# Pool weights two groups to a unit, and the rope key's 32 columns outside the units

## The reference

```
h = rmsnorm(x) * (1 + sc1) + sh1
proj = h @ w_in                     # 1024 x 4128: cq 768 | ckv 256 | kr 32 | u 1024 | gates 2048
latent = [rmsnorm(ckv), rope(kr)]   # kr is the key part shared by all heads
q = rmsnorm(cq) @ w_uq
y[g] = window_mean(u[g], width 2, 4, 8, 16) - u[g]      # 4 groups of 256 channels
a_out = concat_g(y[g] @ w_pool[g]) * pool_scale         # w_pool[g] is 256 x 256
mixed = (sigmoid(gates[:1024]) * a_out + sigmoid(gates[1024:]) * attention) @ w_out
```

## Time and profile before

| | |
|---|---|
| median of three runs | 2399.89 us (2397.15 to 2406.32) |
| profiled execution | 2402.1 us, span 2400.3 us |
| TensorE matmul busy | 2294.3 us, 96% |
| VectorE, ScalarE, GpSimd busy | 48%, 36%, 28% |
| mean granted TensorE clock | 0.973 |
| chain that ended last | PE 87%, DVE 4%, ACT 2%, DMA 2%, SP queue 2%, POOL 1% |
| mean DMA rate | 96 GB/s |

### The profile page before, as it was taken

How to read it: one execution, slowest core, us unless ns; L and a number is a source line. 1 busy time by engine, 2 the same in 40 slices (tenths; PEclk the granted TensorE clock), 3 DMA queues, 4 the chain that set the end, 5 groups by cost and what they waited for, 6 DMA issues and landing times.

```text
span 2400.3 us, 43263 instructions
## 1 busy us (share of the span) xinstructions
PE 2294.3 (96%) x16431; PEld 2058.7 (86%) x16431; DVE 1150.5 (48%) x1701; ACT 867.5 (36%) x1864; POOL 666.6 (28%) x328
## 2 busy tenths in 40 slices
PE   6999999999988999999989999999999889999998
PEld 4889998757768999998988898977676789999998
DVE  3342651743345666651152608337334556666433
ACT  4123224732213555541231222267222235555321
POOL 0233433400003333333322234333000223333332
PEclk8999999999999999999989999999999989999999
DMA  8564332033312222236336542321332222222322
GB/s 282 153 209 85 75 81 64 21 97 95 104 36 70 71 85 81 79 100 183 110 115 195 162 84 70 85 58 29 97 96 76 62 62 79 83 83 79 89 82 80
DMA packets 338370, 230.62 MB, mean 96 GB/s; under 512 B 62828, under 2 KB 321701, under 8 KB 338236
## 3 DMA queue, kind: packets, MB, share of 16 engines
q1 hardware_dynamic: 336034, 224.01, 32.5%
q10 hardware_dynamic: 2202, 4.79, 0.6%
HBM read 223.15 MB, written 5.60 MB: 95 GB/s over the span
## 4 chain that ended last, share of the span: by engine, by line
PE 87%; DVE 4%; ACT 2%; DMA 2%; SPq 2%; POOL 1%; issue 1%; DVEq 1%; ACTq 0%
PE PS L1426 57%; PE PS L1394 6%; PE PS L1786 5%; PE PS L1832 5%; PE PS L1703 3%; PE PS L1443 2%; PE PS L1729 2%; POOL wlo L897 1%; PE PS L1508 1%; PE PS L1706 1%; PE PS L1625 1%; PE PS L1680 1%; DMA raw<-w_in 1%; PE PS L1780 1%; PE PS L1755 1%
## 5 line engine op out<-in xcount | busy, mean ns | idle before, releaser
L897 POOL TENSOR_TENSOR wlo<-raw,whi 128x1024 fp32r<-128x1024 f32 (+2 forms) x260 | 596.4, 2295 | 1610.0 <-ACT whi L507 1610.0
L507 ACT ACTIVATE whi<-raw 128x1024 fp32r<-128x1024 f32 (+2 forms) x260 | 260.1, 1001 | 913.5 <-PE PS L1426 714.7
L1426 PE MATMUL PS<-h_hi,whi 128*128 128x288 f32 (+1 forms) x2528 | 549.0, 299 | 17.1 <-POOL wlo L897 17.1
L1426 PE MATMUL PS<-h_lo,whi 128*128 128x288 f32 (+1 forms) x2528 | 544.9, 297 | 0.0
L1426 PE MATMUL PS<-h_hi,wlo 128*128 128x288 f32 (+1 forms) x2528 | 544.6, 297 | 0.0
L1426 PEld LDWEIGHTS PS<-h_hi,whi 128*128 128x128 f32 (+1 forms) x2528 | 408.6, 189 | 30.7 <-POOL wlo L897 18.3
L1426 PEld LDWEIGHTS PS<-h_hi,wlo 128*128 128x128 f32 (+1 forms) x2528 | 409.8, 189 | 0.7
L1426 PEld LDWEIGHTS PS<-h_lo,whi 128*128 128x128 f32 (+1 forms) x2528 | 409.5, 189 | 0.7
L1327 DVE TENSOR_SCALAR conv<-zext,convp 128x592 f32<-128x592 f32 x88 | 160.5, 1824 | 147.7 <-ACTq L817 147.7
L1426 PE MATMUL PS<-act_hi,whi 128*128 128x288 f32 x704 | 152.8, 298 | 1.6 <-POOL wlo L897 1.6
L1426 PE MATMUL PS<-act_lo,whi 128*128 128x288 f32 x704 | 150.8, 295 | 0.0
(11 more groups left out here) (263 smaller groups left out, 3394.2 us busy)
## 6 DMA issues: line engine op xcount, KB each, us to landing
raw<-w_up SPq DMA_DIRECT2D x88, 512.0 KB, 3.7
pages<-cache_latent SPq DMA_DIRECT2D x256, 144.0 KB, 2.1
raw<-w_in SPq DMA_DIRECT2D x64, 512.0 KB, 4.1
ada_ring<-w_ada SPq DMA_DIRECT2D x64, 512.0 KB, 4.9
raw<-w_down SPq DMA_DIRECT2D x32, 512.0 KB, 3.8
ada_first<-w_ada SPq DMA_DIRECT2D x16, 512.0 KB, 10.0
raw<-w_out SPq DMA_DIRECT2D x16, 512.0 KB, 3.8
ada_next<-w_ada SPq DMA_DIRECT2D x16, 512.0 KB, 3.8
```

The lines of the kernel that those rows point to most:

```text
L507: nc.scalar.activation(whi[:, slot, 0:width(u)], raw[:, slot, 0:width(u)], ACT.Copy).then_inc(hi_ready.sem, 1)
L897: nc.gpsimd.tensor_tensor(wlo[:, slot, 0:n], raw[:, slot, 0:n], whi[:, slot, 0:n].bitcast(F32), ALU.subtract).then_inc(lo_ready.sem, 1)
L1426: r = mm(PS[0:m, 2 * (j % 2) + half, 0:HT], w, o[:, k0 + k, half * HT:half * HT + HT], start=(first and k == 0 and part is whi and o is xh ...
```

## The change

The rope key has no units any more. Its 32 columns of `w_in` are loaded once per layer to a buffer `kr_raw` (128 KB, in pieces of 128 bytes), right behind the `rope` table. TensorE multiplies them in fp32, without splitting the weights, with `h_hi` and with `h_lo`: block k goes to column group k % 4, so four partial sums arise at PSUM partitions 0, 32, 64, 96. ScalarE copies the first, and VectorE adds the other three. The `u` tiles use the other pair of PSUM banks first. On SP the loads of the first `u` units move up to where the rope key's stood.

The pool weights of two groups form one unit of 1024 columns and 48 matmuls (two such units instead of four), and the 18 units of the stage stand in the order of the table `GATE_UNITS`. The gate loops are written out instead of looped.

Of the diff, the parts that the text speaks of:

```
-U_CQ, U_KV, U_KR, U_U = 0, 6, 8, 10
-U_QN, U_QR, U_POOL, U_GB, U_UK, U_UV, U_OUT, U_UP, U_DOWN, UNITS = 18, 26, 30, 42, 50, 52, 54, 62, 106, 130
+U_CQ, U_KV, U_U = 0, 6, 8
+U_QN, U_QR, U_GATE, U_UK, U_UV, U_OUT, U_UP, U_DOWN, UNITS = 16, 24, 28, 46, 48, 50, 58, 102, 126
+GATE_UNITS = (("a", 0), ("a", 1), ("pool", 0), ("a", 2), ("a", 3), ("b", 0), ("b", 1), ("b", 2), ("b", 3), ("pool", 1),
+              ("a", 4), ("a", 5), ("a", 6), ("a", 7), ("b", 4), ("b", 5), ("b", 6), ("b", 7))
...
                 sp.dma_start(rope[:].rearrange("p a b -> p (a b)"), A["rope"]).then_inc(rope_in.sem, 16)
+                sp.dma_start(kr_raw[:].rearrange("p (k n) -> p k n", k=KD), A["w_in"][l, :, C_KR:C_KR + DR].rearrange("(k p) n -> p k n", p=128)).then_inc(kr_in.sem, 16)
...
+                for f in range(2):
+                    u_unit(f)
+                    ring_load(2 * KD + 12 + 2 * f)
+                    ring_load(2 * KD + 13 + 2 * f)
+                for f in range(KD):
                     ring_load(2 * KD + 16 + 2 * f)
                     ring_load(2 * KD + 17 + 2 * f)
+                    if f + 2 < KD:
+                        u_unit(f + 2)
...
-                hi(l, U_KR + 2, 0, 0)
-                act.wait_ge(unit_used.sem, unit_used.at(l, U_KR + 2))
-                nc.scalar.activation(two(krope[:]), PS[0:DR, 0:2, 0:HT], ACT.Copy).then_inc(free["qkv"].sem, 2)
-                hi(l, U_KR + 3, 0, 1)
+                act.wait_ge(kr_p.sem, kr_p.at(l, 1))
+                nc.scalar.activation(two(krope[:]), PS[0:DR, 0:2, 0:HT], ACT.Copy).then_inc(kr_ev.sem, 1)
...
+                for g in range(1, 4):
+                    v.drain()
+                    last = v.tensor_tensor(two(krope[:]), PS[32 * g:32 * g + 32, 0:2, 0:HT], two(krope[:]), ALU.add)
+                last.then_inc(free["qkv"].sem, 2)
...
+                window_mean(1)
+                for m in range(4):
+                    pool_tile(m)
+                v.drain()
+                gated_tile(0)
+                gated_tile(1)
+                window_mean(2)
+                gated_tile(2)
+                gated_tile(3)
+                window_mean(3)
+                for m in range(4, KD):
+                    pool_tile(m)
+                v.drain()
+                for m in range(4, KD):
+                    gated_tile(m)
...
-                for s in range(2):
-                    use(l, U_KR + s)
-                    products(s, 4, h_hi, h_lo, 4 * s, 0, first=s == 0, last=s == 1, m=DR).then_inc(unit_used.sem, 1)
-                    ada_pair(6 + s)
+                for r in range(2):
+                    for o in (h_hi, h_lo):
+                        for half in range(2):
+                            for g in range(4):
+                                k = 4 * r + g
+                                last = mm(PS[32 * g:32 * g + 32, half, 0:HT], kr_raw[:, DR * k:DR * k + DR], o[:, k, half * HT:half * HT + HT].bitcast(F32),
+                                          start=(r == 0 and o is h_hi), stop=(r == 1 and o is h_lo))
+                last.then_inc(kr_p.sem, 1)
+                ada_pair(6)
+                ada_pair(7)
```

More of the change, by code:

```diff
@@ L172, in build @@
     kv_sum = at("kv_sum", [128, 2, T], end_at + 2 * B)
+    kr_raw = at("kr_raw", [128, KD * DR], q_at + 12608)
     rows = at("rows", [128, 17, 128], q_at)
@@ L231, in loads_before @@
     def loads_before(u):
-        return sum(2 if U_QN <= w < U_QR else 4 if U_QR <= w < U_POOL else 1 for w in range(u % 2, u, 2))
+        return sum(2 if U_QN <= w < U_QR else 4 if U_QR <= w < U_GATE else 1 for w in range(u % 2, u, 2))
     def width(u):
-        if U_KR <= u < U_U:
-            return 128
-        if U_QN <= u < U_POOL:
-            return 768
-        if U_POOL <= u < U_GB and (u - U_POOL) % 3 == 0:
-            return 512
+        if U_QN <= u < U_GATE:
+            return 768
         return 768 if U_DOWN <= u and (u - U_DOWN) % 3 == 2 else 1024
@@ L398, in _ @@
                     cq_unit(1)
-                for u in range(2, U_KR):
+                for u in range(2, U_U):
                     cq_unit(u)
@@ L427, in _ @@
                                          .rearrange("p a k h n -> p (a k) (h n)")).then_inc(loaded[s].sem, 16)
[L429 to L437, removed]
+                for i, (kind, m) in enumerate(GATE_UNITS):
+                    u = U_GATE + i
+                    if kind == "pool":
+                        unit(l, u, u % 2, raw[:, u % 2].rearrange("p (k n) -> p k n", k=4),
+                             A["w_pool"][l, 2 * m:2 * m + 2].rearrange("g (k p) n -> p (g k) n", p=128))
+                    else:
+                        c = C_G + 128 * m + (D if kind == "b" else 0)
+                        unit(l, u, u % 2, raw[:, u % 2].rearrange("p (k n) -> p k n", k=8),
+                             A["w_in"][l, :, c:c + 128].rearrange("(k p) n -> p k n", p=128))
                 for w, u0 in ((A["w_uk"], U_UK), (A["w_uv"], U_UV)):
@@ L674, in _, with gate @@
                 tiles(l, U_QR, 4, to_qr)
-                for g in range(4):
-                    u = U_POOL + 3 * g
-                    hi(l, u + 2, 0, u % 2)
[L680 to L690, removed]
+                def gate(kind, m, e):
+                    if kind == "a":
+                        act.wait_ge(gated.sem, gated.at(l, m - 1))
+                        nc.scalar.activation(two(gate_a[:, m % 2, :]), bank_pair(e), ACT.Sigmoid).then_inc(free["g"].sem, 1)
+                    else:
+                        nc.scalar.activation(two(gate_b[:, m, :]), bank_pair(e), ACT.Sigmoid).then_inc(free["g"].sem, 1)
+                for i, (kind, m) in enumerate(GATE_UNITS):
+                    u = U_GATE + i
+                    act.wait_ge(unit_used.sem, unit_used.at(l, u + 1))
+                    hi(l, u + 2, 0, u % 2)
+                    if kind != "pool":
+                        gate(kind, m, GATE_ORDER.index((kind, m)))
                 for p in range(8):
@@ L1163, in _, with pool_tile, gated_tile @@
                 dve.sem_inc(passed[2], 1)
[L1164 to L1175, removed]
+                def pool_tile(m):
+                    dve.wait_ge(full["pool"].sem, full["pool"].at(l, m + 1))
+                    b = 4 + 2 * (m % 2)
+                    v.tensor_scalar(two(uext[:, m, 0:T]), PS[:, b:b + 2, 0:HT], par[:, P_PS + m:P_PS + m + 1], None, ALU.mult).then_inc(free["pool"].sem, 1)
+                def gated_tile(m):
+                    dve.wait_ge(free["g"].sem, free["g"].at(l, GATE_ORDER.index(("a", m)) + 1))
+                    v.tensor_tensor(uext[:, m, 0:T], uext[:, m, 0:T], gate_a[:, m % 2, :], ALU.mult).then_inc(gated.sem, 1)
+                window_mean(1)
[10 more added lines that the diff above has]
+                    pool_tile(m)
+                v.drain()
+                for m in range(4, KD):
+                    gated_tile(m)
                 v.drain()
```

63 lines of the change are left out of this document (30 added, 33 removed).

## The result

The changed kernel takes 2365.56 us (median of four runs, 2359.77 to 2366.62). The kernel before takes 2398.98 us in the same comparison (2397.15 to 2406.32). The ratio is 0.9855, with a 95% interval of 0.9836 to 0.9874: faster by 33.4 us by the medians (30.2 to 39.3 by the interval of the ratio). The forecast was 2367 us.

A forecast was written before the change was run, and what follows sets the result against it. TensorE was taken to bound the kernel, with waits at the rope key and gate stage. Gains of 18.8 + 13.1 + 1.1 = 33.0 us took the profiled 2402.1 to 2369.1, median about 2367 us; range 2360 to 2373.

The forecast's parts named there:

- The stage of gates: Pool and gate units: 125.10 us become 18 units of 6.43, 115.7 us; gain 9.4 us a layer, 18.8 in all.
- VectorE in time: Window means ready for both pool units: 1.5 us to spare at the first, at worst a few tenths late at the second.
- The rope key: Rope key in fp32 on four column groups: 64 entries in 4.2 us, range 4.0 to 4.4.
- The loads: Earlier `u` loads on SP leave the path; with the fp32 rope key the stretch becomes 12.8 us, gaining 13.1 in all.
- third `u` load: On SP behind four ring loads: issued near 120, landing near 127, `wlo` done near 131, wanted at about 134.
- Second wait: Layer 1, fourth `u` product to transposes: 36.5 us become 35.4, gain 1.1 us, possibly 0.
- `kr_raw`: Its 128 KB load ahead of layer 0's first two `w_in` loads delays ScalarE's `whi` 0 to 1.5 us; taken as 0.
- written-out loops: Gate loops written out make more program for TensorE; cost taken as 0 because `gate_a` matmuls already run so at the same pace.
- Serial groups: Rival at the rope key: column groups run one behind the other, 17.8 us, whole kernel 2394 us; chance 0.04.
- each entry is finished before the next starts: Rival at the rope key: 0.43 us an entry, 27.7 us in all, whole kernel slower at 2414 us; chance 0.03.
- The clock did not fall in the narrow stretch: Rival denied here: rope key and two pairs lower the clock, 4 us a layer, whole kernel 2375 us; chance 0.09.
- No unit waited: Rival denied here: VectorE or the third `u` load late, 2 to 3 us a layer lost, 2376 us; chance 0.06.

The follow-up runs named there:

- kernel with the gates alone: Kernel before with only the doubled pool units and the new gate stage order, rope key and loads as before; 2383.03 us against 2396.13, ratio 0.9939.
- kernel with the pool unit at the head: Changed kernel with the two pool units at places 0 and 5 of `GATE_UNITS` instead of 2 and 9; 2429.16 us, ratio 1.012 to the kernel before.
- kernel with the loads alone: Kernel before, narrow split rope key kept, with each `u` load one pair (two ring loads) earlier on SP; 2387.98 us against 2396.13, ratio 0.9963.
- rope key alone: Kernel before with only the fp32 rope key, its loads and their new order, pool units and gates as before; 2382.13 us against 2396.13, ratio 0.9945.
- run with one group: Changed kernel with all eight rope key blocks accumulated on one column group, without VectorE's three additions; 2386.8 us against 2397.66 for the kernel before.
- old load order: Changed kernel with the `u` loads put back where they stood on SP; 2407.98 us against 2396.13 for the kernel before, ratio 1.0047.

## Why the prediction was right

**The stage of gates.** Forecast 115.7 us, measured 116.1; a gain of 9.0 for 9.4. The difference is no more than two times 0.26 us behind the pool units, which I did not count. The kernel with the gates alone shows the same stage by itself.

**VectorE in time.** I forecast 1.5 us to spare at the first pool unit. Window mean 1 is done at 264.92, and the third tile is due near 264.33 + 3.17 = 267.5, so it was 2.6 us, and TensorE shows no wait there. For the second I allowed a few tenths of lateness. VectorE's last part of mean 3 (`304.18` + 3.70) ends at 307.88, before the pool unit begins at 309.58, and its third tile comes 3.2 us later still. Counted from the start of the stage, I had mean 2 begin at 21.9 us and mean 3 end at 59.5. They did so at 23.7 (275.17 - 251.50) and at 56.4: the means began later than forecast, but took 13.8 and 17.5 us, where I had given them their longest times, 16.2 and 19.8. So the two errors worked against each other. How real the danger is the kernel with the pool unit at the head shows, some 60 us in the two stages.

```profile
275.17 1.62 DVE L1138 TENSOR_TENSOR win<-uext 128x1420 f32<-128x1420 f32 x1
304.18 3.70 DVE L1157 TENSOR_TENSOR y_lo<-win,y_hi 128x1024 fp32r<-128x1024 f32 x3
```

**The rope key.** Forecast 4.2 us (4.0 to 4.4), measured 3.88, just below the lower end. It was counted from the fp32 entries of the earlier trace rows with 12.5% more columns; at 62 ns for one of four side by side, 64 entries without the factor give 3.97. The Trainium skill, TensorE: Matmul & The Clock Gate, section "Measured speedup vs the span model", gives 2.38 for three column tiles, by which I had estimated 5.3 us; the trace does not agree: 15.5 / 3.88 = 4.0 for four groups, with 288 columns where the page has N = 512. The sum did not rest on it.

**The loads.** The load of the first `u` unit has left the chain in both layers, as forecast, and with it the low clock of the product behind. (The first two `u` loads moved by two pairs each, not by one and two as the prediction says; the places it gives them are right.) The third `u` load was forecast to be issued near 120 and was issued at 120.89; its `whi` ran at 128.15 without a wait of TensorE. The kernel with the loads alone shows that this step carried most of the rope key's half. What the working did not see is how much hung on it: with the fp32 rope key, with ScalarE's list as it is and without the new order, the kernel is slower than before (2408 us).

**Second wait and `kr_raw`.** From the end of the fourth `u` product (1304.46 + 6.60) to the transposes in layer 1 it is 35.4 us, which was the forecast; the gain is 1.1 us. In layer 1's chain:

```profile
1346.45 1.13 PE PS L1407 x6
```

The load of `kr_raw` shows no cost: the first products of layer 0 begin at 59.08 us in the changed kernel, at 58.73 in the kernel with the gates alone, which has no such load, and at 56.23 in the one with the rope key alone, which has it. It was 55.78 before. What goes with the later start is the gates' half, as said above; the prediction put the written-out loops at 0 by the pace of the matmuls alone, and that term may be where these 2 us belong.

**The rivals.** Serial groups would have made the rope key 15 us and longer; the run with one group shows how that looks, 2387 us. That each entry is finished before the next starts did not happen either. The clock did not fall in the narrow stretch: 1.00 over 115.6 to 121.4, and even in the 15 us of narrow work of the run with one group the profile gives 1.00. No unit waited, and no pair in this trace; the 0.8 to 1.4 us of a pair's wait for its ring load, in other kernels with this order, is the nearest to it.

**Sum.** 33.0 us forecast for the parts of the change, 33.3 by the milestones, 33.4 by the medians. The forecast of 2367 was 1.4 us above the result. The parts of the sum came out one by one, within 0.4 us a layer for the stage and 0.6 for the rope key's stretch. That the three totals agree to 0.4 us is partly chance: the profiles differ besides by the 4.3 us of attention and the 1.9 of the start, of which the working had neither, and the interval of the ratio is 9 us wide.

## What to carry to other kernels

A late load costs what stands behind the instruction that waits for it, on that instruction's own engine, and what waits for that in turn; follow the list past the waiting instruction before you price it (42 us here, where the load alone was worth 16). When two edits come together, ask of each what the other one would do without it: here the rope key in fp32 gained nothing without the earlier `u` loads, and with ScalarE's list as it was the pair was a loss. And a unit that is made larger wants more of its inputs at once, so its place in the order has to be paid for by what fills the time before it.

## What the runs showed of the hardware beyond that

- Narrow fp32 work on one column group costs 0.242 us an entry with 32 x 288, and four groups side by side take the same time for four entries (3.88 us for 64): no loss to the different weights and tiles was seen.
- Small VectorE operations are at times 2 us longer than their like while GpSimd writes a `wlo`: `win<-win,ramp` 128 x 30 took 0.19 us or 2.22 us. In the changed kernel three of six were of the long kind, the one of window mean 3 among them:

```profile
299.22 2.22 DVE L1142 TENSOR_TENSOR win<-win,ramp 128x30 f32<-128x30 f32 x1
```

  All three lie over a `wlo` and end 0.04 to 0.06 us behind its end (301.44 behind 301.40, for example); the three short ones fall where GpSimd is idle. That looks like a wait for the `wlo` to end. I only saw the two side by side; no run took GpSimd's work away to test it.
- The first rope key matmuls behind the 8.3 us gap of the old load order ran at half pace (16 in 2.15 us against 1.15, at a granted clock of 0.50), and so did a part of the first product behind other gaps (8.55 against 6.59 us for 48). But the two gate units behind the first pool unit, 14.52 us in the kernel before, took 13.08 in the kernels with the loads alone and with the rope key alone, with the same 3.53 us of `wlo` ahead of them. So a gap of that length does not always cost the low clock, and what decides it stays open.
